# A three-layer block kernel on Trainium2: layer one's gate, query and key projections in one block, and a new order of clears, maxima and context outputs in the first attention

## The reference

```python
def block(qi):
    s = jnp.einsum('bqgrd,bsgd->bgrqs', qi, k).astype(jnp.float32) * scale
    p = jax.nn.softmax(s, axis=-1).astype(v.dtype)
    return jnp.einsum('bgrqs,bsgd->bqgrd', p, v)
```

```python
qk, v, o, g = split_cols(jnp.dot(h, w_in), ODD_SPLITS)
q, k = jnp.split(jax.nn.silu(dwconv(qk, conv_w, conv_b)), 2, axis=-1)
g = (g + gate_b).astype(jnp.float32).reshape(B, T, 4, MLSTM_HEADS)
gates = (g[0], jax.nn.log_sigmoid(g[1]), g[2], jax.nn.log_sigmoid(g[3]))
```

## Time and profile before

| | |
|---|---|
| median of 3 executions | 3152.98 us (3152.7 to 3154.68) |
| profiled execution | 3153.24 us, its span 3151.5 us |
| TensorE busy | 2794.8 us, 89% of the span |
| VectorE, ScalarE, GpSimd busy | 46%, 33%, 5% |
| attention block | from 276.3 to 545.5 us of the span |
| gate block, query and key block | from 1356 to 1473.8 us |

### The profile page before, as it was taken

One profiled execution on the slowest core, in us unless ns is written; L12 is line 12 of the kernel. 1 busy time (PEld: TensorE's weight loads), 2 busy tenths in 40 slices (PEclk: granted clock), 3 DMA queues, 4 the chain that ended last, 5 costly groups with the idle time before them and its releaser, 6 DMA issues. The chain is left out here.

```text
span 3151.5 us, 33505 instructions
## 1 busy us (share of the span) xinstructions
PE 2794.8 (89%) x13718; PEld 2207.9 (70%) x13718; DVE 1463.6 (46%) x1822; ACT 1024.7 (33%) x1292; POOL 151.2 (5%) x93
## 2 busy tenths in 40 slices
PE   7986988799999999759988889998987499999998
PEld 5863555578888888437966677886665278777886
DVE  5236676644333232663145354343759743343332
ACT  5242333523212122633245342232322333232221
POOL 0211121000000000000000000000130100000000
PEclk9997999999999999979999899999898799999999
DMA  6010000712111111622100122322120022221321
GB/s 244 19 65 14 1 1 1 280 43 78 54 67 54 54 57 64 254 90 76 68 2 1 54 94 74 108 76 98 67 74 27 14 97 95 75 94 65 116 77 64
DMA packets 36303, 232.75 MB, mean 74 GB/s; under 512 B 4048, under 2 KB 5072, under 8 KB 12624
## 3 DMA queue, kind: packets, MB, share of 16 engines
q1 hardware_dynamic: 36176, 230.96, 20.5%
HBM read 228.85 MB, written 2.10 MB: 73 GB/s over the span
## 5 line engine op out<-in xcount | busy, mean ns | idle before, releaser
L323 PE MATMUL pair<-h_high,w_high 128*128 128x512 f32 x2016 | 731.9, 372 | 55.3 <-ACT w_high L265 28.8
L324 PE MATMUL pair<-h_low,w_high 128*128 128x512 f32 x2016 | 724.5, 368 | 0.0
L277 DVE TENSOR_TENSOR w_low<-ring,w_high 128x2048 fp32r<-128x2048 f32 (+5 forms) x222 | 472.4, 2134 | 368.9 <-ACT w_high L265 368.7
L265 ACT ACTIVATE w_high<-ring 128x2048 fp32r<-128x2048 f32 (+5 forms) x225 | 398.5, 1774 | 362.9 <-PE pair L329 219.7
L323 PEld LDWEIGHTS pair<-h_high,w_high 128*128 128x128 f32 x2016 | 384.4, 191 | 127.5 <-issue 30.6
L329 PE MATMUL pair<-h_high,w_low 128*128 128x512 f32 x2016 | 448.6, 365 | 0.0
L324 PEld LDWEIGHTS pair<-h_low,w_high 128*128 128x128 f32 x2016 | 384.9, 191 | 65.7 <-issue 2.2
L329 PEld LDWEIGHTS pair<-h_high,w_low 128*128 128x128 f32 x2016 | 350.2, 189 | 61.9
L323 PE MATMUL pair<-high,w_high 128*128 128x512 f32 (+1 forms) x768 | 286.6, 382 | 24.8 <-DVEq L1013 15.7
L324 PE MATMUL pair<-low,w_high 128*128 128x512 f32 (+1 forms) x768 | 279.6, 373 | 0.0
L323 PEld LDWEIGHTS pair<-high,w_high 128*128 128x128 f32 x768 | 148.2, 193 | 54.7 <-issue 23.0
(11 more groups left out here) (384 smaller groups left out, 3722.8 us busy)
## 6 DMA issues: line engine op xcount, KB each, us to landing
ring<-in_w_up SPq DMA_DIRECT2D x66, 1024.0 KB, 4.8
ring<-in_w_ada SPq DMA_DIRECT2D x32, 1024.0 KB, 5.2
ring<-in_w_down SPq DMA_DIRECT2D x32, 704.0 KB, 4.0
ring<-in_w_ada0t SPq DMA_DIRECT2D x16, 1024.0 KB, 4.9
ring<-in_w_merge SPq DMA_DIRECT2D x16, 1024.0 KB, 4.8
ring<-in_w_down SPq DMA_DIRECT2D x8, 1024.0 KB, 4.8
ring<-in_w_att_in SPq DMA_DIRECT2D x6, 1024.0 KB, 6.6
ring<-in_w_heads SPq DMA_DIRECT2D x6, 1024.0 KB, 4.8
```

What stands on the lines that cost most here:

```text
L265: self.nc.scalar.activation(self.w_high[:, n % 2, 0:floats], self.ring[:, chunk % RING, 0:floats], ACT.Copy).then_inc(self.high_ready.sem, 1)
L277: (on or self.nc.vector).tensor_tensor(self.w_low[:, n % 2, 0:floats], self.ring[:, chunk % RING, 0:floats], self.w_high[:, n % 2, 0:float ...
L323: self.nc.tensor.matmul(out[:, a:e], w_high[:, k, at], high[:, k, a:e], start=k == 0, stop=False)
L324: self.nc.tensor.matmul(out[:, a:e], w_high[:, k, at], low[:, k, a:e], start=False, stop=False)
```

## The change

In the attention:

- `peak_piece` reads 96 rows (even GQA units) or 128 rows (odd ones) where it read the 64 rows of data; the rest is zero. So the extra row of an odd unit's queries (row 0) must be zero again before its pieces, and GpSimd clears it in units 3, 5 and 7.
- `top_row` makes all 128 output rows alike, where it made one, and ScalarE copies the one it needs from its own partition.
- VectorE keeps 5 of its 10 clears; the 2 that the first pieces need come first, and the maxima of unit 0 are behind all 5. GpSimd does the clears of the odd buffer, two of them only when it has done the low parts of unit 0, and the three of unit 8. ScalarE waits for no clear any more.
- VectorE's order in a unit is now: divide the latents, all 7 maxima and the join of the next unit, then the context output of the unit before. This is done for every unit, and `value_step(u, 6)` waits for the context output of unit u-1.

In layer one, `gate_stage` and `conv_qk_stage` become one block, `gate_conv_stage`. Both halves of the gates are one product of 128 outputs. It opens together with the first two products of the keys; keys come before queries, and a third product buffer replaces a fourth. VectorE's gate work lies between the convolutions.

```diff
+                b, r = u % 2, full(u)
+                    if u == 0:
+                        pe.wait_ge(ones_ready.sem, ones_ready.base + 2)
+                    elif odd(u):
+                        pe.wait_ge(cleared.sem, cleared.base + blanks(u))
...
-                if s == 6 and u >= 2 and u % 2 == 0:
+                if s == 6 and u >= 1:
-                    pe.wait_ge(ctx_normed.sem, ctx_normed.base + u // 2)
+                    pe.wait_ge(ctx_normed.sem, ctx_normed.base + u)
...
-            act.wait_ge(ones_ready.sem, ones_ready.base + 1)
             stage_high(0)
...
+                if u + 1 < UNITS:
+                    for n in range(PEAKS):
                         reduce_max(u + 1, n)
                     join_max(u + 1)
+                if u > 0:
+                    invert_ctx(u - 1)
                     chain.sync()
-                    scale_ctx(u - 2)
                     scale_ctx(u - 1).then_inc(ctx_normed.sem, 1)
...
+            chain.step(nc.gpsimd.memset(k_high[0:64, 1, :].bitcast(F32), 0.0))
+            nc.gpsimd.memset(k_high[0:1, 1, :].bitcast(F32), 1.0).then_inc(cleared.sem, 1)
+            nc.gpsimd.memset(q_high[0:64, 1, :].bitcast(F32), 0.0).then_inc(cleared.sem, 1)
             for u in range(UNITS):
+                if odd(u) and u > 1:
+                    pool.wait_ge(probed.sem, probed.base + STEPS * (u - 1))
+                    nc.gpsimd.memset(q_high[0:1, 1, :].bitcast(F32), 0.0).then_inc(cleared.sem, 1)
...
+            K.opening(pe, [(gates, g, 0, P, gate_done), (product_of(0), first, 0, P, done),
+                           (product_of(1), first, 1, P, done)], norm)
+            for p in range(2, 8):
+                if p >= 3:
+                    pe.wait_ge(conved.sem, conved.base + p - 2)
+                K.product(pe, product_of(p), first + p // 2, KD, 256, p % 2, K.h_high, K.h_low,
+                          cols_of(p)).then_inc(done.sem, 1)
+            pe.wait_ge(keys_ready.sem, keys_ready.base + 1)
...
+            norm.dve(dve, chain, both_low)
+            dve.wait_ge(gate_done.sem, gate_done.base + 1)
...
+            K.split_low(dve, first + 1)
+            conv(0)
+            conv(1)
+            K.split_low(dve, first + 2)
...
+            scan_context(run, gx, ALU.add)
+            conv(2)
+            scan_latents(run, gx, ALU.add)
...
+            conv(3)
+            K.split_low(dve, first + 3)
+            scan_context(high, gi, ALU.max)
+            conv(4)
+            scan_latents(high, gi, ALU.max)
+            conv(5)
+            K.split_low(dve, first + 4)
...
+            conv(6)
+            conv(7)
```

More of the change, by code:

```diff
@@ L1548, in score_step @@
                     pe.wait_ge(lows.sem, lows.base + u + 1)
+                    if u == 0:
+                        pe.wait_ge(ones_ready.sem, ones_ready.base + 3)
                 if g >= 2:
@@ L1677, in _ @@
             for u in range(UNITS + 1):
-                ahead, pair_done = u + 1 < UNITS, u > 0 and u % 2 == 0
                 if u > 0:
@@ L2321, in layer0, with gate_conv_stage @@
     ffn(K, 0, ALL, 5, K.v("norm2_0", 0, 8), scale=4, shift=3)
-def gate_stage(K, keysT, floorT, top, norm):
+QK_ORDER = [4, 5, 6, 7, 0, 1, 2, 3]
+def gate_conv_stage(K, qT, kT, keysT, floorT, top, norm):
     nc = K.nc
-    g = K.first("w_ml_gate")
-    w_parts = K.parts(g, KD, P)
-    K.begin_split(["w_ml_gate"])
+    g, first = K.first("w_ml_gate"), K.first("w_ml_qk")
+    done, gate_done, turned = K.pe_a, K.pe_b, K.pe_c
+    tap, silu, soft_ready, floor_ready = K.act_a, K.act_b, K.act_c, K.act_d
+    conved, gate_read, keys_ready, tops_ready = K.dve_a, K.dve_b, K.dve_c, K.dve_d
+    cw, cb = VEC["mcw"][0], VEC["mcb"][0]
+    K.begin_split(["w_ml_gate", "w_ml_qk"])
     R = 64
+    gates, turns = K.pairs[3], K.pairs[3]
+    product_of = lambda p: K.pairs[p % 3]
+    parts_of = lambda p: spans(ALL) if QK_ORDER[p] >= 4 else [(0, LAT)]
+    cols_of = lambda p: parts_of(p)[-1][1]
     with ExitStack() as stack:
@@ L2382, in _ @@
             chain.sync()
-            nc.scalar.activation(soft[:], soft[:], ACT.Ln, bias=K.ones[0:R, 0:1]).then_inc(K.act_a.sem, 1)
-            act.wait_ge(K.dve_c.sem, K.dve_c.base + 1)
-            nc.scalar.activation(soft[:, 0:LAT], gx[:, 0:LAT], ACT.Exp, scale=-1.0).then_inc(K.act_b.sem, 1)
+            nc.scalar.activation(soft[:], soft[:], ACT.Ln, bias=K.ones[0:R, 0:1]).then_inc(soft_ready.sem, 1)
+            for p in range(8):
+                middle_tap(p)
+                if p % 2 == 1:
+                    act.wait_ge(done.sem, done.base + p + 1)
+                    K.split_high(act, first + p // 2 + 2)
+                finish(p)
+            act.wait_ge(tops_ready.sem, tops_ready.base + 1)
+            nc.scalar.activation(soft[:, 0:LAT], gx[:, 0:LAT], ACT.Exp, scale=-1.0).then_inc(floor_ready.sem, 1)
             chain.close()
@@ L2391, in _ @@
             chain = Chain(dve, K.dve_chain)
-            K.split_fresh_low(dve)
-            norm.dve(dve, chain)
-            K.split_low(dve, g + 1)
-            chain.step(nc.vector.memset(zero[:], 0.0))
-            dve.wait_ge(K.pe_a.sem, K.pe_a.base + 1)
-            chain.step(nc.vector.tensor_scalar(gi[:], K.pairs[0][0:R, 0:ALL], K.v("gate_i", rows=R), None, ALU.add))
-            nc.vector.tensor_scalar(gx[:], K.pairs[1][0:R, 0:ALL], K.v("gate_f", rows=R), None,
-                                    ALU.add).then_inc(K.dve_a.sem, 1)
@@ L2401, in _, with both_low, conv @@
-            dve.wait_ge(K.act_a.sem, K.act_a.base + 1)
+            def both_low():
+                K.split_fresh_low(dve)
+                K.split_low(dve, first)
+            def conv(p):
+                dve.wait_ge(tap.sem, tap.base + p + 1)
+                b, ps = QK_ORDER[p], product_of(p)
+                for a, e in parts_of(p):
+                    chain.step(nc.vector.scalar_tensor_tensor(
+                        buf[:, p % 2, a + 1:e], ps[:, a:e - 1], K.vec[:, cw + b:cw + b + 1],
+                        buf[:, p % 2, a + 1:e], ALU.mult, ALU.add))
+                chain.sync()
+                for a, e in parts_of(p):
+                    op = nc.vector.scalar_tensor_tensor(
+                        buf[:, p % 2, a:e - 1], ps[:, a + 1:e], K.vec[:, cw + 16 + b:cw + 17 + b],
+                        buf[:, p % 2, a:e - 1], ALU.mult, ALU.add)
+                op.then_inc(conved.sem, 1)
@@ new lines, in _, with scan_context @@
+            ways = ((slice(0, 32), 1, ALL - 1), (slice(32, 64), -1, LAT))
+            part = lambda x, r, rev, a, e: x[r, a:e] if rev == 1 else x[r, a:e][:, ::-1]
+            def scan_context(out, data, op):
+                for r, rev, _ in ways:
+                    chain.step(nc.vector.tensor_tensor_scan(part(out, r, rev, LAT, ALL), part(zero, r, rev, LAT, ALL),
+                                                            part(data, r, rev, LAT, ALL), 0.0, ALU.add, op))
+                chain.sync()
@@ new lines, in scan_latents @@
+            def scan_latents(out, data, op):
+                for r, rev, last in ways:
+                    chain.step(nc.vector.tensor_tensor_scan(part(out, r, rev, 0, LAT), part(zero, r, rev, 0, LAT),
+                                                            part(data, r, rev, 0, LAT), out[r, last:last + 1],
+                                                            ALU.add, op))
+                chain.sync()
+            chain.step(nc.vector.memset(zero[:], 0.0))
+            norm.dve(dve, chain, both_low)
@@ new lines, in _ @@
+            dve.wait_ge(gate_done.sem, gate_done.base + 1)
+            nc.vector.tensor_scalar(gx[:], gates[R:2 * R, 0:ALL], K.vec[R:2 * R, VEC["gate_f"][0]:VEC["gate_f"][0] + 1],
+                                    None, ALU.add).then_inc(gate_read.sem, 1)
+            chain.step(nc.vector.tensor_scalar(gi[:], gates[0:R, 0:ALL], K.v("gate_i", rows=R), None, ALU.add))
+            K.split_low(dve, first + 1)
+            conv(0)
+            conv(1)
+            K.split_low(dve, first + 2)
+            dve.wait_ge(soft_ready.sem, soft_ready.base + 1)
```

201 lines of the change are left out of this document (60 added, 141 removed).

## The result

The changed kernel takes 3095.64 us, the median of four executions (3092.72 to 3100.75), and the kernel before 3152.95 in the same batch (3152.7 to 3154.68). The ratio is 0.9819, with a 95% interval of 0.9802 to 0.9836. The forecast was 3095. The profiled execution of the changed kernel took 3092.72 us (span 3090.9), which is 60.5 less than the profiled one of before, where 58.2 were forecast.

A forecast was written before the change was run, and what follows sets the result against it. Attention's start and every second unit wait for VectorE; layer one's gate chain leaves TensorE idle. Attention 22.7 (6.6 + 13.9 + 2.2) plus layer one 35.5 is 58.2 us: 3153.2 to 3095, range 3086 to 3107.

The forecast's parts named there:

- The attention's start: Clears at the attention's start: ScalarE copies at once and the first join ends its wait earlier, 6.6 us gained.
- the bound of 4.4: Attention's start: lower bound of the gain, if GpSimd's three first clears held up VectorE's by 2.1 us.
- The periods: Attention units 1 to 15: fourteen periods of 14.3 us, 200.2 instead of 214.1, 13.9 us less.
- the wait for the context: Each attention unit: TensorE waits 0.9 us at the context values for VectorE's context output, 13.37 + 0.9 = 14.3.
- The first period and the end: Attention: first period loses about 0.8, last gains the 0.9 wait, nothing in sum; one context output fewer at the end, 2.2 less.
- the drains: Attention's first period: a few idle gaps at weight loads of 64-row pieces go, about 0.8 us at the low clock.
- Layer one: Merged block: gate chain hidden by products 1 to 7 and a changed opening; next block starts 35.5 us earlier.
- The tail: Layer one's end: 6.8 us between the last product and the next block, 4.56 before.
- The rivals: Context wait worse, 3112 (8%); VectorE bounds block, 3100 to 3105 (12%); no overlap, 3115 (3%); slower, 3284 (2%); more, 3083 to 3089 (4%).
- the fall of the clock: Rival in the attention: the new waits let TensorE's clock fall to 1.2 GHz, up to 189 us more, 3284; 2%.
- the end's 2.2 us: Attention's end: only one context output is left instead of two, 1.77 + 0.43 = 2.2 us less.
- six wider weight loads: Attention's row of maxima, 128 outputs alike: the wider loads lie under the 0.9 us wait.

The follow-up runs named there:

- the later kernel without the wait for the context: The change with unit u-1's context values put behind unit u's first scores in TensorE's order: 3086.08 us, ratio 0.9786.
- layer one alone: The changed kernel with the attention of before, so only the merged layer one block is new: 3118.88 us, ratio 0.9893.
- the kernel with contexts in pairs: The change with VectorE's old order: context outputs of two units between the maxima of every second unit; wide row kept: 3111.66 us, ratio 0.9867.
- the narrow one: The kernel with contexts in pairs and old VectorE order, its row of maxima one output row instead of 128: 3100.52 us, ratio 0.9831.
- the shallow pieces: The change with the GQA units' pieces reading 64 rows again: 3103.08 us, ratio 0.9841.
- unit 8's clears: The change with the three clears for unit 9's rows on VectorE and ScalarE's copies waiting for them: 3104.70 us, ratio 0.9842.
- the two kernels with before's attention: The kernel before, 3152.95 us, and the changed kernel with before's attention put back, 3118.88 us.

## Why the prediction was right

*The attention's start* was put at 6.6 us and measured at 6.64 in the change, and at 6.65 when it was undone. GpSimd's clears beside VectorE's held up neither (they take 0.73 and 0.70 us, and the five of VectorE are over in 4.12, from 277.85 to 281.97, against 0.83 for each of before's ten), so the bound of 4.4 had no part. By the Trainium skill's "SBUF — State Buffer", section "SBUF: two separate sides", VectorE locks the port pair that it shares with GpSimd in a two-port mode, or with two inputs in SBUF against a GpSimd instruction that reads SBUF. A clear reads nothing, so the second case can't arise here, and the trace shows no sign of the first.

*The periods* were put at 14.3 and came out at 14.33. The reason holds too: the later kernel without the wait for the context has 13.51, so the wait costs 0.82 us in a period, forecast 0.9. MLA units gained next to nothing (0.2), since 14.38 in each replaces 13.37 and 15.47 in turn. The rest of the 13.4 us comes from GQA units (5.6) and from units 8 and 9 (7.6).

*The first period and the end.* From the first join to the second extra row are 0.8 us less than before, which is what the prediction named for the drains. But chance can do as much there: the first period of before's attention, at a low clock, is 16.91 us in one trace and 15.77 in that of layer one alone. From the last extra row to the last context product are 20.01 us instead of 21.52, so 1.5 less: one context output of 2.2, less the new wait. In all the attention is 22.4 us shorter (268.66 less 246.26), against 22.7.

*Layer one* was put at 35.5 and gained 35.3. With the block's start 26.7 us earlier than in the trace before, the steps were forecast at 1357.1 for the last tile, 1360.6 for the gates and 1404.5 for the last product; they came at 1357.3, 1361.2 and 1405.2. The tail was 6.6 (last product's end at 1405.2), forecast 6.8. TensorE's idle time in the opening was 1.10 us and not 2 to 3, and the clock did not fall there. The products had no gap from 1351.89 to the last.

*The total.* The two blocks gained 57.7 us, forecast 58.2, and that is the agreement that counts. That the median came within 0.6 us of the forecast is luck in part: its four executions spread over 8.0 us. The 60.5 of the profiled executions is so too: 2.8 of it lie in stages of the same code (5.4 less between the two blocks, some 2.6 more elsewhere).

*The rivals.* None came about in the change. But two of the arguments against them were weaker than I wrote. Against the fall of the clock I set the waits of up to 2 us at a clock of 1.00 before, as if their length decided; the kernel with contexts in pairs has the same 1.82 us, and the clock falls behind five of seven. The Trainium skill's "TensorE: Matmul & The Clock Gate", section "A second HAM failure mode: psum-queue depth-cycling", tells of a kernel with such swings between groups of matmuls; the kernel with contexts in pairs shows them, and the kernel before, with idle times as long, does not. The change has no such dips, and its waits are shorter (0.45 us before the matmul); that this is why isn't shown. The order, which the prediction valued at the end's 2.2 us and little in the periods, is worth 16 us in the attention beside the wide row and 4 beside the narrow one. And the six wider weight loads were costed at nothing under the 0.9 us wait. That was right for the change (200.4 against 200.7), and wrong for any kernel in which the wait is gone.

What stays open is why the clock falls more often behind the wide row. The kernels show that it does, and not by what.

## What to carry to other kernels

An instruction that waits for another engine's late result is best followed through its queue: 0.8 us of scores moved in front of the wait gave 12 us. Clears that one engine does ahead of everybody's first work hold up all of it: here five of ten on an idle engine, and the others out of the way of the first copy and pieces, gave 6.6 us, and GpSimd's share cost nothing. When parts of a change are undone one at a time, their worths need not add up: the shallow pieces (7.5), the old order (12.6, over half of it dips) and unit 8's clears (6.7) lose 26.8 us in the periods, where all of them together had gained 13.4. So read each in its stage, and compare stages, not medians, once the effect is below the spread of executions.

## What the runs showed of the hardware

- A granted clock of 1.00 behind a wait of 1.82 us does not mean that such a wait is safe. Six matmuls with 128-column weights behind it (0.88 us) were followed by slow matmuls in five of seven cases (clock 0.50 for some 3 us in the one shown), the same with one-column weights (0.52 us) in one of seven, and in none of seven in the two kernels with before's attention.
- A 128-column broadcast in place of one column costs 0.36 us for six matmuls (0.88 against 0.52).
- Three clears of GpSimd (0.73 us each) beside five of VectorE (0.70 each) held up neither.
- Stages of identical code took 806.1 to 814.9 us in fourteen traces. Between two that are 7.3 us apart the granted clocks differ by 0.02 to 0.03 in single windows.
